# Seven block products for eight in the feed-forwards of a two-block layer stack (one NeuronCore)

## The reference

```python
D_FF = 2816
def _swiglu(x, w1, w3, w2):
    return (jax.nn.silu(x @ w1) * (x @ w3)) @ w2

x = _layernorm(DEEPNORM_ALPHA * x + 0.5 * _swiglu(x, ffn1_w1, ffn1_w3, ffn1_w2), ln1_g, ln1_b)
m = _mixer(x, ...)
x = _layernorm(DEEPNORM_ALPHA * x + m, ln2_g, ln2_b)
x = _layernorm(DEEPNORM_ALPHA * x + 0.5 * _swiglu(x, ffn2_w1, ffn2_w3, ffn2_w2), ln3_g, ln3_b)
```

## Time and profile before

| | |
|---|---|
| median of three runs | 3948.86 us (3948.81 to 3955.92) |
| profiled execution: span of its instructions | 3945.0 us |
| what the median has beside that span | 3.9 us |
| TensorE busy | 3484.9 us, 88% |
| VectorE, ScalarE, GpSimd busy | 1899.4 us (48%), 1151.9 us (29%), 80.0 us (2%) |
| ffn1 in the trace | about 1851.6 to 2586 us |
| ffn2 in the trace | about 3172 to 3945 us (the end) |

### The profile page before, as it was taken

The page is one execution under the profiler, slowest core; times in us unless marked ns, Lnnn a source line. Parts: engine busy times, 40 slices in busy tenths (PEclk is TensorE's granted clock), DMA queues, the critical chain, the costliest instruction groups (busy, mean ns, idle before and its releaser), DMA issues. The chain is left out here.

```text
span 3945.0 us, 67598 instructions
## 1 busy us (share of the span) xinstructions
PE 3484.9 (88%) x30402; PEld 2794.9 (71%) x30402; DVE 1899.4 (48%) x2705; ACT 1151.9 (29%) x1713; POOL 80.0 (2%) x91
## 2 busy tenths in 40 slices
PE   2999899999757777779999999989967989999997
...
DMA packets 141692, 284.70 MB, mean 72 GB/s; under 512 B 8156, under 2 KB 81004, under 8 KB 141148
## 3 DMA queue, kind: packets, MB, share of 16 engines
...
...
## 5 line engine op out<-in xcount | busy, mean ns | idle before, releaser
L242 DVE TENSOR_TENSOR ring_b_wl<-ring_b_raw,ring_b_wh 128x1024 fp32r<-128x1024 f32 (+1 forms) x200 | 236.5, 1183 | 1112.9 <-ACT ring_b_wh L239 1112.9
L274 PE MATMUL PS<-ffn_x_high,ring_b_wh 128*128 128x512 f32 x1408 | 551.0, 391 | 13.1 <-DVE ffn_x_low L537 9.5
L239 ACT ACTIVATE ring_b_wh<-ring_b_raw 128x1024 fp32r<-128x1024 f32 (+1 forms) x200 | 204.6, 1024 | 1181.3 <-PE PS L276 1169.5
L276 PE MATMUL PS<-ffn_x_high,ring_b_wl 128*128 128x512 f32 x1408 | 549.2, 390 | 0.0
L275 PE MATMUL PS<-ffn_x_low,ring_b_wh 128*128 128x512 f32 x1408 | 549.0, 390 | 0.0
L274 PEld LDWEIGHTS PS<-ffn_x_high,ring_b_wh 128*128 128x128 f32 x1408 | 265.2, 188 | 73.8 <-issue 9.5
L276 PEld LDWEIGHTS PS<-ffn_x_high,ring_b_wl 128*128 128x128 f32 x1408 | 265.0, 188 | 55.3
L275 PEld LDWEIGHTS PS<-ffn_x_low,ring_b_wh 128*128 128x128 f32 x1408 | 265.2, 188 | 54.9 <-issue 0.2
L274 PE MATMUL PS<-ffn_hid_high,ring_b_wh 128*128 128x512 f32 x704 | 275.1, 391 | 2.6 <-DVE ring_b_wl L242 2.6
L276 PE MATMUL PS<-ffn_hid_high,ring_b_wl 128*128 128x512 f32 x704 | 273.9, 389 | 0.0
L275 PE MATMUL PS<-ffn_hid_low,ring_b_wh 128*128 128x512 f32 x704 | 273.9, 389 | 0.0
...
## 6 DMA issues: line engine op xcount, KB each, us to landing
...
```

The costliest lines, as they stand in the source:

```text
L239: return nc.scalar.activation(out, x, ACT.Copy)
L242: return nc.vector.tensor_tensor(out, x, high.bitcast(fp32), ALU.subtract)
L274: nc.tensor.matmul(out, wh, xh, start=k == 0, stop=False)
L276: last = nc.tensor.matmul(out, wl, xh, start=False, stop=k == kt - 1)
```

## The change

The up projections of hidden tiles 2 to 21 are computed by the Winograd form of Strassen's scheme: the 2x2 block matrix A (rows: gate tile and value tile; columns: input features 0 to 511 and 512 to 1023) times the 2x2 block matrix B (rows: the same feature halves; columns: token chunks 0 and 1). Seven products of 128 x 512 by 512 x 512 stand for eight, each of 4 k-steps x 3 = 12 matmuls. Hidden tiles 0 and 1 stay plain (`plain`). The differences of weight blocks (four per hidden tile, `sums`) are made by GpSimd, in the memory that holds the blocks; those of the input rows (T1 to T4) once per feed-forward, by VectorE and GpSimd. The products are joined by seven adds from PSUM on VectorE (`combine`) and one copy on ScalarE; Silu then reads SBUF.

The down projection is no longer gathered over eight hidden tiles. Hidden tile u is multiplied as soon as the products of tile u + 2 run: eight blocks (`down_block`: one k-step, 2 chunks, 6 matmuls each) are put between the seven products (`BLOCKS_AFTER`), in two pairs of PSUM banks, and each is added to `xT` by VectorE (`update`). The last two hidden tiles (for chunk 1 the last four) are kept for a tail that works chunk by chunk as before. The bias of the norm ahead of ffn2 is added by ScalarE. Down weights are laid out by hidden tile on the host. Up weights come as four DMAs of 128x512 per hidden tile, into a ring of 11 slots.

```diff
+            N_PLAIN = 2
+            QUADS = range(N_PLAIN, KF)
+            B11, B21, T1, T2, T3, T4, B22 = range(7)
+            PRODUCTS = (("A11", B11), ("S2", T2), ("S1", T1), ("S3", T3), ("A12", B21), ("A22", T4), ("S4", B22))
+            BANK_READ = ((-1, 2), (-1, 5), (-1, 6), (-1, 7), None, (0, 1), (0, 4))
...
+            SUMS_FOR = {"A11": 3, "S2": 4, "S1": 2, "S3": 3, "A12": 4, "A22": 1, "S4": 4}
...
+            BLOCKS_AFTER = {q: (1, 1, 2, 1, 2, 1, 0) for q in QUADS}
+            BLOCKS_AFTER[N_PLAIN] = (0, 0, 1, 2, 2, 1, 2)
...
+                def await_slot(eng, q, w):
+                    j = allocation(q, w)
+                    if j >= N_SLOTS:
+                        was = j - N_SLOTS
+                        eng.wait_ge(prod.h, prod.base + number(N_PLAIN + was // 7, PLACE[ALLOC[was % 7]]) + 1)
...
+                        def load_quad(q):
+                            for w in ("A11", "S3", "A12", "A22"):
+                                half, k = BLOCKS[w]
+                                await_slot(sp, q, w)
+                                sp.dma_start(slot(q, w), w_up[2 * q + half][:, k:k + KH, :]).then_inc(raw_in[q % 2].h, 16)
...
+                            load_quad(q)
+                        sp.wait_ge(prod.h, prod.base + number(KF - 1, 1) + 1)
+                        load_down(KF - 2)
+                        load_down(KF - 1)
...
+                        def sums(q):
+                            done = sums_done.base + 4 * (q - N_PLAIN)
+                            pool.wait_ge(raw_in[q % 2].h, raw_in[q % 2].base + 64 * ((q - N_PLAIN) // 2 + 1))
+                            a11, a12, a21, a22 = (slot(q, w) for w in ("A11", "A12", "S3", "A22"))
+                            s1, s2, s4 = (slot(q, w) for w in ("S1", "S2", "S4"))
+                            await_slot(pool, q, "S1")
+                            nc.gpsimd.tensor_tensor(s1, a21, a22, ALU.add).then_inc(sums_done.h, 1)
+                            await_slot(pool, q, "S2")
+                            pool.wait_ge(sums_done.h, done + 1)
+                            nc.gpsimd.tensor_tensor(s2, s1, a11, ALU.subtract).then_inc(sums_done.h, 1)
+                            nc.gpsimd.tensor_tensor(a21, a11, a21, ALU.subtract).then_inc(sums_done.h, 1)
+                            await_slot(pool, q, "S4")
+                            pool.wait_ge(sums_done.h, done + 2)
+                            nc.gpsimd.tensor_tensor(s4, a12, s2, ALU.subtract).then_inc(sums_done.h, 1)
+
+                        sums(2)
...
+                        def product(q, i):
+                            w, o = PRODUCTS[i]
+                            n = number(q, i)
+                            pe.wait_ge(cut_low.h, cut_low.base + n - 4 * N_PLAIN + 3)
+                            if q == N_PLAIN:
...
+                                pe.wait_ge(bank_read.h, bank_read.base + i // 2 + 1)
+                            else:
+                                back, at = BANK_READ[i]
+                                pe.wait_ge(combined.h, combined_at(q + back, at))
+                            out, wh, wl = up_bank(q, i), highs[(n - 4 * N_PLAIN) % 4], rest(q, w)
+                            for k in range(KH):
+                                nc.tensor.matmul(out, wh[:, k, :], xh[:, o, k], start=k == 0, stop=False)
+                                nc.tensor.matmul(out, wh[:, k, :], xl[:, o, k], start=False, stop=False)
+                                last = nc.tensor.matmul(out, wl[:, k, :], xh[:, o, k], start=False, stop=k == KH - 1)
+                            last.then_inc(prod.h, 1)
...
+                        def down_block(q, m):
+                            u, n = q - 2, block_count(q) + m
+                            pe.wait_ge(down_low.h, down_low.base + u + 1)
+                            pe.wait_ge(hid_low.h, hid_low.base + max(4, gate_count(u, 1)))
+                            if n >= 2:
+                                pe.wait_ge(updated.h, updated.base + n - 1)
+                            else:
+                                pe.wait_ge(multiplied.h, multiplied.base + 4)
+                            out = block_banks(q, m)
+                            last = down([u], m, 0, out[:, 0:512])
+                            if q < FIRST_LATE + 2:
+                                last = down([u], m, 1, out[:, 512:1024])
+                            last.then_inc(blocks_done.h, 1)
+
...
+                        for q in QUADS:
+                            m = 0
+                            for i in range(7):
+                                product(q, i)
+                                for _ in range(BLOCKS_AFTER[q][i]):
+                                    down_block(q, m)
+                                    m += 1
...
+                        for q in QUADS:
+                            for i in range(7):
+                                n = number(q, i)
+                                if i == 0:
+                                    act.wait_ge(prod.h, prod.base + n + 1)
+                                    act.wait_ge(hid_low.h, hid_low.base + (gate_count(q - 1, 0) if q > N_PLAIN else 4))
+                                    nc.scalar.activation(unit(0), two(up_bank(q, 0)), ACT.Copy).then_inc(copied.h, 1)
+                                if i == 4:
+                                    act.wait_ge(combined.h, combined_at(q, 5))
+                                    nc.scalar.activation(unit(0), unit(0), ACT.Silu).then_inc(silu_done.h, 1)
+                                cut(n + 4)
+                                if q == N_PLAIN and i == 1 and biased_in:
+                                    act.wait_ge(x_low.h, x_low.base + 4 * len(LOW_ORDER))
...
+                                    hidden_high(q, 1, 1)
+                        cut_down(KF - 2)
+                        cut_down(KF - 1)
 
                         def biased(c):
                             t, w = MAIN_CHUNKS[c]
                             for k in range(KD):
...
+                        def combine(out, x, q, i):
+                            nc.vector.tensor_tensor(out, x, two(up_bank(q, i)), ALU.add).then_inc(combined.h, 1)
+
+                        def gate(q, c, x, up, ready):
...
+                        for q in QUADS:
+                            m = 0
+                            for i in range(7):
+                                n = number(q, i)
+                                if i in (1, 3, 4, 5, 6):
+                                    dve.wait_ge(prod.h, prod.base + n + 1)
+                                if i == 1:
+                                    dve.wait_ge(copied.h, copied.base + q - N_PLAIN + 1)
+                                    dve.wait_ge(hid_low.h, hid_low.base + (gate_count(q - 1, 1) if q > N_PLAIN else 4))
+                                    combine(unit(1), unit(0), q, 1)
+                                elif i == 3:
+                                    dve.wait_ge(combined.h, combined_at(q, 1))
+                                    combine(unit(2), unit(1), q, 3)
+                                    dve.wait_ge(combined.h, combined_at(q, 2))
+                                    combine(unit(3), unit(2), q, 2)
+                                    combine(unit(1), unit(1), q, 2)
+                                elif i == 4:
+                                    combine(unit(0), unit(0), q, 4)
+                                elif i == 5:
+                                    combine(unit(2), unit(2), q, 5)
+                                    gate(q, 0, unit(0), unit(2), 6)
+                                elif i == 6:
+                                    dve.wait_ge(combined.h, combined_at(q, 4))
+                                    combine(unit(1), unit(1), q, 6)
+                                cut(n + 4)
+                                for _ in range(BLOCKS_AFTER[q][i]):
+                                    update(q, m)
+                                    m += 1
+                                if i == 3 and q < KF - 1:
+                                    cut_down(q - 1)
+                                if i == 6:
+                                    gate(q, 1, unit(1), unit(3), 7)
+                                    hidden_low(q, 0, 0)
+                                    hidden_low(q, 1, 1)
+                        cut_down(KF - 2)
...
-        a[f"ffn{n}_down"] = tiles(g[f"ffn{n}_w2_2"][0])
+        a[f"ffn{n}_down"] = g[f"ffn{n}_w2_2"][0].reshape(KF, P, D)
...
+    nc = bacc.Bacc("TRN2", target_bir_lowering=False, num_devices=1, dynamic_dma_scratch_size=1024)
```

536 lines of the change are left out of this document (391 added, 145 removed).

## The result

The changed kernel took 3917.05 us (median of 4 runs, 3913.7 to 3921.2) against 3948.84 for the kernel before (4 runs on the same chip, 3942.8 to 3955.92): ratio 0.9923, 95% interval 0.9907 to 0.9939. It is faster by 31.8 us, where 77 were forecast.

A forecast was written before the change was run, and what follows sets the result against it. Both feed-forwards were taken as bound by TensorE's number of matmuls. The terms, -108.8 + 17 + 12.8 - 6.5 + 6 + 3 = -76.5 us, gave 3872 us in time (forecast range 3862 to 3888, widest 3850 to 3919).

The forecast's parts named there:

- Term 1: Up projections of both feed-forwards: 480 fewer matmuls at 0.227 us each, -108.8 us.
- rival (e): TensorE pays 0.05 us at each of 15 boundaries per tile, 24 us, giving 3896; chance 0.20 shared with slow GpSimd sums.
- Term 2: Steady hidden tiles: chain through GpSimd's sums stalls TensorE 0.35 us plus 0.1 contention, over 38 tiles +17 us (0 to +64).
- p: Time of one GpSimd sum in the hidden tiles, taken as 1.34 us, between 0.90 and 1.78.
- the formula: TensorE's stall per hidden tile without contention: 2p - 2.3 us, forecast as 0.35.
- under 0.8 us each: Sign of being right: TensorE's steady waits, once per hidden tile ahead of its last down block, stay under 0.8 us.
- own sign for (c): Sign of being wrong: VectorE's low parts in the steady part take much over 0.69 us.
- Rival (c): VectorE shut out for a whole GpSimd instruction, one meeting per tile: 1.65 x 38 = 63 us, 3918; chance 0.05.
- Term 3: Hand-over after each feed-forward's last product: TensorE waits 6.4 us for hidden halves and two down low parts, +12.8 us.
- Terms 4 to 6: Feed-forward start -6.5 us; ScalarE's bias add in ffn2 +6 (0 to 8.5); chunk-by-chunk tail +3 (0 to 8).
- Term 4: Feed-forward start: four plain tiles on chunk 0 precede chunk 1, where two did, -6.5 us (0 to -8).
- taken as 0: Late cutting of the first products' weights at the start, bounded by 5 us per feed-forward, counted as nothing.

The follow-up runs named there:

- e1: Changed kernel with VectorE's low part of the down weights moved from after the fourth to after the sixth product's updates: 3869.71 us, 0.9805 to the kernel before.
- e7: Changed kernel with GpSimd's fourth sum waiting until VectorE has made the tile's down-weights low part: 3880.95 us, 0.9837 to the kernel before.
- the phases above: Ahead of the changed kernel's work, four VectorE instructions beside idle GpSimd, two-operand sums or one-operand instructions: two-SBUF-operand VectorE 2.50 to 6.78 us beside sums; whole 4000.85.
- e2: Changed kernel with GpSimd making the third sum ahead of the second: 3873.77 us, 0.9828 to the kernel before.
- e5: Changed kernel with the last two hidden tiles' down weights cut among the last tile's products instead of after it: 3906.50 us, 0.9905 to the kernel before.
- e6: Changed kernel with ScalarE adding ffn2's bias rows two by two over four steps instead of all eight at once: 3905.11 us, 0.9899 to the kernel before.

## Why the prediction was wrong

The time, 3917, lies inside the widest range, at its upper end, but the gain is 31.8 us where 77 were forecast. The busy time by stretch gives the bill (window, length, PE busy and so on). Before:

```profile
1853.70:2587.80 734.10, 725.91 (x3179) 597.40 (x3179) 213.83 (x216) 137.26 (x144) 0.09 (x1) 1.00 0.17 52
3167.30:3945.00 777.70, 743.62 (x3208) 602.23 (x3206) 240.73 (x236) 157.97 (x168) 28.26 (x16) 0.99 0.17 53
```

The changed kernel:

```profile
1860.30:2574.80 714.50, 681.75 (x2939) 553.10 (x2939) 559.55 (x658) 199.09 (x314) 121.94 (x89) 0.99 0.15 49
3153.00:3915.70 762.70, 700.67 (x2968) 561.66 (x2967) 575.34 (x682) 228.77 (x346) 117.30 (x88) 0.97 0.15 50
```

e1, in which the stall is gone:

```profile
1854.60:2546.50 691.90, 675.36 (x2939) 553.82 (x2939) 539.20 (x658) 199.26 (x314) 122.54 (x89) 0.99 0.15 51
3124.90:3867.90 743.00, 696.41 (x2968) 562.97 (x2966) 562.22 (x682) 228.94 (x346) 117.87 (x88) 0.97 0.15 52
```

The two stretches together went from 1511.8 to 1477.2 (-34.6), and to 1434.9 in e1 (-76.9). The rest of the kernel was 5.3 us longer in the changed kernel's profiled run, which gives the span's -29.3.

**Term 1** stands: 480 matmuls fewer, still 0.227 apart. The boundaries between products cost nothing visible (e1's tiles take just their 132 matmuls), so rival (e) is out.

**Term 2 is the step that failed**, and in it one number: "0 to 0.43 us; I take 0.1 as the mean" for the down weights' low part meeting the fourth sum. It is 0.84, in 34 tiles of 38 and near it in three. +17 us were forecast, 42.3 measured (changed less e1), 25 of the 42 us that are missing in the stretches (76.5 less 34.6). p was right (1.30), the chain's other pieces too (stall 0.24 in e7, 0.30 by the formula; with the 1.34 that was taken for p the formula gives 0.38, not the 0.35 in the forecast, a slip of 1 us), and the place of the wait, once per tile ahead of the last down block, as well; "under 0.8 us each" was not. Both my bounds came from a row with a one-operand instruction on GpSimd, which the phases above show to be much milder than a two-operand sum. The low part was also not late by chance: the product that starts the fourth sum and the one that starts VectorE's combines stand in a fixed order, so a meeting that happens once happens in nearly every tile, and a mean over chances was the wrong form. The prediction's own sign for (c), VectorE's low parts much longer than they should be, was there to see, though on the down weights' low part and not on those of 0.69.

**Rival (c)** named this mechanism and its time, 3918, with a chance of 0.05. The price was not quite its own: it charged a whole sum (1.30) on top of 0.35, where 0.84 came on top of 0.24. That its 3918 meets 3917 so closely is luck: its 63 us for term 2 are 21 too many, and the other terms were 17 too few. The Trainium skill (SBUF — State Buffer, Who interferes with whom) says that a VectorE instruction with two SBUF inputs and a GpSimd one that reads SBUF block each other for the whole instruction, whichever comes first having its way. The sums nearly agree, in both orders: 1.22 became 2.06 in the changed kernel, 1.29 became 1.90 in e2, each 0.14 to 0.15 short of the whole rest of the other instruction and its own time. The one-operand phases do not agree, as full blocking of four VectorE instructions would cost more than the 0.6 to 0.8 us seen. I held L537's 0.74 beside a GpSimd TENSOR_SCALAR against the rule; what it refuted was only that case.

**Term 3** was right for the gap (6.2 against 6.4 us, twice), and for what ends it, the two down low parts behind the hidden low part. e5 confirms their 2.6.

**Terms 4 to 6 and what was not in the sum.** Without the stall, everything but the matmuls cost 108.8 - 76.9 = 31.9 us, where +15.3 was forecast (12.8 - 6.5 + 6 + 3). TensorE's idle time rose by 8.4 us in ffn1 and 12.5 in ffn2 (length less busy, e1 less before): 20.9, of which the hand-over is 12.4 and the bias, by e6, about 5. Term 4's gain of 6.5 at the start did not come: in ffn2 the plain products wait 4.2 us and a later product 4.4 for its weights' low part, which I had "taken as 0", where products waited 9.5 before; in ffn1 a down block waits 2.2 us for the first down weights' low part. The other 11 us are in busy time (it fell by 97.8, the matmuls are 108.8), and the clock accounts for them: behind new gaps come new stretches at the lower level. Two slices of the changed kernel, around the hand-over in ffn1 and at the start of ffn2:

```profile
2520.00:2530.00 10.00, 3.83 (x11) 2.80 (x10) 5.59 (x7) 5.57 (x7) 0.00 (x0) 0.66 0.30 105
...
3210.00:3220.00 10.00, 5.55 (x20) 4.15 (x19) 10.00 (x13) 7.63 (x14) 3.59 (x3) 0.79 0.30 105
```

0.66 and 0.79 are means of the two levels, 2.4 and 1.2 GHz, in a slice in which TensorE stood for 6.2 and 4.5 us. Summed over all parts of the two stretches in which the granted clock is 0.50 (length, then TensorE's busy time), first before, then e1:

```profile
sum 26.20, PE 12.37 PEld 7.61 DVE 18.32 ACT 13.00 POOL 3.40; mean PE 3.09 PEld 1.90 DVE 4.58 ACT 3.25 POOL 0.85
sum 65.10, PE 37.84 PEld 23.95 DVE 48.15 ACT 31.49 POOL 0.07; mean PE 3.78 PEld 2.40 DVE 4.82 ACT 3.15 POOL 0.01
```

So 25.5 us more of busy time lie at the lower level, where a matmul takes 0.43 us for 0.227: that costs 12 us, an estimate from these rows, against the 11 to be explained. No run held the clock fixed to test it.
